# Decode attention: when the pages of the second and third set and the second rotary group are gathered

## The chip, the cores and the metric

The kernel runs on one core of a Trainium2 chip. The metric is the device time of one launch in microseconds, as the median of several runs. The five engines of the core (TensorE, VectorE, ScalarE, GpSimd and SyncE) run their own instruction streams and meet at semaphores; GpSimd and SyncE also issue the transfers. In the rows of the profile they are PE (PEld is the weight load of PE), DVE, ACT, POOL and SP.

## What is computed

One layer of a hybrid decoder: layer norm, one input projection, a gated linear attention head group, a latent attention (MLA) head group, an output projection and a gated feed-forward network with a short convolution. It is computed for a prompt of 1024 tokens with 16 meta tokens ahead of them, and for 8 decode sequences of 4 tokens. The change touches the seam between the two latent attentions:

```python
# prompt: causal attention per head over the prompt's own keys
s = (einsum('bthc,bsc->bhts', ql, ckv) + einsum('bthr,bsr->bhts', qr, krope)) * MLA_SCALE
p = softmax(where(kpos <= pq, s, NEG_INF));  o = einsum('bhts,bsc->bthc', p, ckv)
...
# decode: 8 sequences, 4096 past positions each, held in pages of 128 positions
past_ckv = cache_ckv[page_table].reshape(Bd, -1, MLA_KV_LORA)     # 256 wide
past_kr  = cache_krope[page_table].reshape(Bd, -1, MLA_ROPE)      # 32 wide
s_past = einsum('bthc,bsc->bhts', q_lat, past_ckv) + einsum('bthr,bsr->bhts', q_rope, past_kr)
p = softmax(concatenate([s_past * MLA_SCALE, s_new], -1))
o = einsum('bhts,bsc->bthc', p[..., :P], past_ckv) + einsum('bhts,bsc->bthc', p[..., P:], ckv_new)
```

All arithmetic is fp32.

## The kernel before

The program is one hand-ordered list of instructions per engine, in eight stages (a to h). Stage d is the attention over the prompt, stage e the attention of the decode tokens over the paged cache. There is no scheduler: the order on an engine is the order of the code, and an engine goes on when the semaphore that it waits for has come to its count.

**Stage d** has `N_ATT` = 66 score steps. Steps 0 and 1 are the last query rows of all heads. Steps 2 to 65 go through four passes of 16 steps; pass p takes heads 2p and 2p+1 over the eight query tiles in the order 7, 0, 6, 1, 5, 2, 4, 3. PE computes the scores of a step (L1298) and counts it in `score_done`; DVE takes the row maxima (L1419), ACT the exponentials (L1359), PE turns the probabilities (L1312), ACT and DVE copy them out, and PE multiplies them with the values (L1335). So heads 0 to 3 have been read for the last time when `score_done` is 34, and all heads when it is 66.

**Stage e** goes through `SETS` = 16 sets. A set is four sequences by 512 positions, loaded as four gathers (pieces b = 0 to 3) on the queue of POOL; each gather reads 128 rows of 4 KB, so 512 KB, into one quarter of a ring slot `ring_c` (L1564, `load_latents`). There are three slots. Slot 0 lies apart; slot 1 lies over the queries `qT` of heads 0 to 3, slot 2 over those of heads 3 to 7. `slot_free` (L1545) holds the loads of a set back until its slot is free: set 1, and by POOL's order all behind it, until `score_done` is 66; set z of 3 and more until the values of set z-3 are computed (`spv_done`). The rotary keys come in four groups of four sets (`load_rotary`, L1568), each in four gathers of 256 KB into `ring_r`, whose slots lie over tensors that are dead before the scores begin. DVE packs one set's share of a group into `ring_p` (L1859).

For a set, PE turns the pages in two parts of `turn_set` (L1652; the first part needs pieces 0 and 1, semaphore `set_loaded`, and ends with the packed rotary keys and the first block of piece 2, which needs `late_loaded`, pieces 2 and 3). ACT and DVE copy the turned blocks out, and PE computes the scores (L1673, `ss_done`) and the values (L1699). This repeats once a set.

What orders the loads in `pool_e` (L1590 to L1616): set 0 during the projections of stage d, the first rotary group at the end of them, the second rotary group when `score_done` is 33, sets 1 and 2 at the end of the scores, set 2 also after `ss_done` is 2 (the two score steps over the new tokens). From set 3 on the four pieces of a set are spread: piece 0 when the slot is free, piece 1 after the scores of set z-2, piece 2 after three, piece 3 after six of the nine turned blocks of set z-1. SP loads the output projection's weights beside this (L1578).

Of the kernel before, what the change touches and what calls it, by code (L numbers as in the profile page):

```python
# [102 lines left out]
def build(nc, ins, outs):  # L103
    with ExitStack() as ctx:
# [8 lines left out]
        def sem(name):  # L113
            return ctx.enter_context(nc.semaphore(name))
# [935 lines left out]
        def out_of_psum(eng, key):  # L1050

            eng.wait_ge(prep_act, act_at[index[key] + 1])
            if dve_at[index[key] + 1]:
                eng.wait_ge(prep_dve, dve_at[index[key] + 1])
# [177 lines left out]
        score_done = sem("score_done")  # L1232
# [14 lines left out]
        N_ATT, N_JOBS = len(att_steps), len(att_jobs)  # L1247
# [239 lines left out]
        SLOTS = 3  # L1487
        SETS = DEC_B // 4 * N_PAGES // 4
# [49 lines left out]
        def step_of(z):  # L1538
            return z + 2
# [5 lines left out]
        def slot_free(eng, z):  # L1545
            if z == 0:

                eng.wait_ge(prep_done, index[("ckv", NT - 1)] + 1)
                eng.wait_ge(latent_stored, 96)
            if z == 1:  # L1550

                eng.wait_ge(score_done, N_ATT)
            if z >= SLOTS:

                eng.wait_ge(spv_done, step_of(z - SLOTS) + 1)

        def rows_of(z, b):
            j = 2 * (4 * (z // 8) + b) + z % 8 // R_SETS
            return bass.IndirectOffsetOnAxis(ap=row_at[:, j, z % R_SETS:z % R_SETS + 1], axis=0)

        def load_latents(z, pieces=range(4)):
            for b in pieces:
                done = (set_loaded if b < 2 else late_loaded)[z % SLOTS]
                nc.gpsimd.indirect_dma_start(ring_c[z % SLOTS][:, b, :, :].rearrange("p j c -> p (j c)"), None,  # L1564
                                             ins["cache_ckv"].rearrange("n (p j) c -> (n p) (j c)", j=4),
                                             rows_of(z, b)).then_inc(done, 16)

        def load_rotary(q, pieces=range(4)):  # L1568
            for b in pieces:
                j = 2 * (4 * (q // 2) + b) + q % 2  # L1570
                nc.gpsimd.indirect_dma_start(ring_r[q % R_SLOTS][b // 2][:, b % 2, :, :].rearrange("p m c -> p (m c)"), None,
                                             ins["cache_krope"].rearrange("n (p j) c -> (n p) (j c)", j=16),
                                             bass.IndirectOffsetOnAxis(ap=rope_at[:, j:j + 1], axis=0)
                                             ).then_inc(rope_loaded[q % R_SLOTS], 16)
# [15 lines left out]
        def pool_e(pool):  # L1590
            pool.wait_ge(pages_ready, 2)
            slot_free(pool, 0)
            load_latents(0)
            out_of_psum(pool, prep[-1])
            load_rotary(0)
            pool.wait_ge(score_done, N_ATT // 2)
            load_rotary(1)
            for z in range(1, SETS):
                slot_free(pool, z)
                if z == 2:  # L1600
                    pool.wait_ge(ss_done, 2)
                if z < SLOTS:
                    load_latents(z)
                    continue
                load_latents(z, (0,))
                if 4 <= z < 12:
                    q = 1 + z // 4
                    if z % 4 == 0:
                        pool.wait_ge(rope_packed, R_SETS * (q - 1))
                    load_rotary(q, (z % 4,))  # L1610
                pool.wait_ge(ss_done, step_of(z - 2) + 1)
                load_latents(z, (1,))
                pool.wait_ge(past_turned, N_TURN * (z - 1) + 3)
                load_latents(z, (2,))
                pool.wait_ge(past_turned, N_TURN * (z - 1) + SPLIT_TURN)
                load_latents(z, (3,))  # L1616
# [1486 lines left out]
        @block.gpsimd  # L3103
        def _(pool):
            pool_ab(pool)
            pool_c(pool)
            pool_e(pool)
            pool_f(pool)
            pool_g(pool)
            pool_h(pool)  # L3110

            for i in range(XS):
                pool.wait_ge(h_stored[i], 16 * (3 if i == 0 else 2))
            pool.wait_ge(state_stored, 32)
            pool.wait_ge(last_state_stored, 16)
            pool.wait_ge(latent_stored, 96 + 48)
            nc.gpsimd.drain().then_inc(end, 1)
# [26 lines left out]
```

## Times and profile before

| what | us |
|---|---|
| median of 3 runs | 1561.29 |
| lowest and highest of them | 1558.99 and 1563.45 |
| the profiled execution, its own time | 1547.4 |
| span of the profiled execution, first to last instruction | 1545.6 |
| PE busy in it | 1479.5 |

The profile is of one execution. Its own time is 1547.4 us, of which 1.8 lie outside the span. It is 13.9 us below the median of the timed runs. All durations below are of this execution; times of day in it count from the first instruction.

### The profile page before, as it was taken

The numbers are of one execution on the slowest core, as the hardware profiler recorded it, in microseconds if no ns is written. First come the engines' busy times: TensorE is split into PE (matmuls) and PEld (weight loads), VectorE is DVE, ScalarE is ACT, GpSimd is POOL, SyncE is SP. The second block draws the span as 40 slices with busy tenths as digits, with TensorE's granted clock in tenths as the row PEclk, the third lists the DMA queues.
The fourth block names the chain that finished last, engine by engine and source line by source line (L and its number), as shares of the span: only waits on it lengthen the run. The fifth ranks groups of instructions, "written<-read, shape, count | busy, mean of one in ns | idle before, by whom it ended". The sixth has DMA issues, their size and how long they took to land.

```text
span 1545.6 us, 29086 instructions
## 1 busy us (share of the span) xinstructions
PE 1479.5 (96%) x11025; PEld 1253.8 (81%) x11025; DVE 1000.2 (65%) x1730; ACT 659.5 (43%) x1236; POOL 364.3 (24%) x395
## 2 busy tenths in 40 slices
PE   5999999999899999999999999999999999999995
PEld 5989999656566666666888999999999998778884
DVE  6714411765555555556678888888888984356587
ACT  2255422543356653334223644555554442435340
POOL 2101000210000014440111244444444442110006
PEclk9999999899899999999999999999999999999998
DMA  7221101200101037774223355555555547978552
GB/s 253 93 70 60 55 28 42 73 28 32 41 2 28 1 126 250 244 253 166 82 95 98 111 180 174 191 183 171 174 180 178 173 167 246 356 248 307 171 191 109
DMA packets 121349, 217.63 MB, mean 141 GB/s; under 512 B 10938, under 2 KB 67896, under 8 KB 118408
## 3 DMA queue, kind: packets, MB, share of 16 engines
q1 hardware_dynamic: 98138, 120.89, 24.3%
q0 software_dynamic: 22976, 95.43, 17.8%
q8 instruction: 62, 1.02, 0.3%
q14 instruction: 29, 0.24, 0.0%
q10 hardware_dynamic: 144, 0.07, 0.0%
HBM read 165.66 MB, written 50.69 MB: 140 GB/s over the span
## 4 chain that ended last, share of the span: by engine, by line
PE 62%; DVE 6%; issue 2%; ACT 2%; DMA 1%; POOL 0%; SPq 0%; DVEq 0%; ACTq 0%; POOLq 0%
PE ps L2312 9%; PE ps L2311 9%; PE ps L2310 9%; PE ps L1298 4%; PE ps L2971 3%; PE ps L2973 3%; PE ps L2972 3%; PE ps L1673 3%; PE ps L210 2%; PE ps L211 2%; PE ps L212 2%; PE ps L1335 2%; PE ps L1652 2%; PE ps L1699 2%; PE ps L1312 2%
## 5 line engine op out<-in xcount | busy, mean ns | idle before, releaser
L2310 PE MATMUL ps<-t_hi,op_hi 128*128 128x266 f32 (+1 forms) x672 | 192.3, 286 | 2.4 <-DVE gap_hi L2534 2.4
L2312 PE MATMUL ps<-t_hi,op_lo 128*128 128x266 f32 (+1 forms) x672 | 192.8, 287 | 0.0
L2311 PE MATMUL ps<-t_lo,op_hi 128*128 128x266 f32 (+1 forms) x672 | 192.7, 287 | 0.0
L210 PE MATMUL ps<-w_hi,hT_hi 128*128 128x256 f32 (+2 forms) x504 | 141.9, 282 | 3.3 <-DVE hT_lo L327 3.3
L2312 PE MATMUL ps<-h1T_hi,op_lo 128*128 128x266 f32 x504 | 144.1, 286 | 0.0
L2311 PE MATMUL ps<-h1T_lo,op_hi 128*128 128x266 f32 x504 | 143.4, 285 | 0.0
L2310 PE MATMUL ps<-h1T_hi,op_hi 128*128 128x266 f32 x504 | 143.4, 284 | 0.0
L212 PE MATMUL ps<-w_hi,hT_lo 128*128 128x256 f32 (+2 forms) x504 | 141.1, 280 | 0.0
L211 PE MATMUL ps<-w_lo,hT_hi 128*128 128x256 f32 (+2 forms) x504 | 141.1, 280 | 0.0
L2767 DVE TENSOR_TENSOR ring_lo<-d_raw,ring_hi 128x1024 fp32r<-128x1024 f32 x77 | 93.5, 1223 | 60.2 <-ACT ring_hi L2763 59.2
L2763 ACT ACTIVATE ring_hi<-d_raw 128x1024 fp32r<-128x1024 f32 x77 | 81.6, 1060 | 114.6 <-DMA d_raw<-t_res 58.9
L2310 PEld LDWEIGHTS ps<-t_hi,op_hi 128*128 128x128 f32 x672 | 127.6, 190 | 2.6 <-DVE gap_hi L2534 2.6
L2311 PEld LDWEIGHTS ps<-t_lo,op_hi 128*128 128x128 f32 x672 | 127.8, 190 | 0.0
L2312 PEld LDWEIGHTS ps<-t_hi,op_lo 128*128 128x128 f32 x672 | 127.4, 190 | 0.0
L2971 PE MATMUL ps<-ring_hi 128*128 128x512 f32 x308 | 122.3, 397 | 4.1 <-DVE ring_lo L2767 3.3
L2972 PE MATMUL ps<-ring_lo,ring_hi 128*128 128x512 f32 x308 | 120.7, 392 | 0.0
L2973 PE MATMUL ps<-ring_hi,ring_lo 128*128 128x512 f32 x308 | 120.6, 392 | 0.0
L2435 DVE TENSOR_TENSOR op_lo<-s_sum,op_hi 128x512 fp32r<-128x512 f32 x84 | 106.1, 1302 | 0.0
L1564 POOL DMA_INDIRECT ring_c<-in_cache_ckv,row_at x64 | 60.2, 940 | 177.1 <-PE ps L1298 69.9
L210 PEld LDWEIGHTS ps<-w_hi,hT_hi 128*128 128x128 f32 x504 | 97.0, 192 | 3.8 <-DVE hT_lo L327 3.7
L212 PEld LDWEIGHTS ps<-w_hi,hT_lo 128*128 128x128 f32 x504 | 97.2, 193 | 0.0
L211 PEld LDWEIGHTS ps<-w_lo,hT_hi 128*128 128x128 f32 x504 | 96.7, 192 | 0.0
(369 smaller groups left out, 3583.2 us busy)
## 6 DMA issues: line engine op xcount, KB each, us to landing
f_raw<-in_w_ffn_in SPq DMA_DIRECT2D x88, 256.0 KB, 3.4
g_res<-gap_lo SPq DMA_DIRECT2D x22, 528.0 KB, 3.6
g_mix<-in_w_down POOLq DMA_DIRECT2D x11, 1024.0 KB, 5.3
t_res<-g_mix POOLq DMA_DIRECT2D x11, 1024.0 KB, 4.2
g_mix<-g_res POOLq DMA_DIRECT2D x11, 1024.0 KB, 5.3
s_res<-g_mix POOLq DMA_DIRECT2D x11, 1024.0 KB, 4.2
d_raw<-in_w_down SPq DMA_DIRECT2D x22, 512.0 KB, 7.2
d_raw<-s_res SPq DMA_DIRECT2D x44, 256.0 KB, 3.7
```

The source lines that it names most:

```text
L210: nc.tensor.matmul(out, ah, bh, start=start, stop=False)
L211: nc.tensor.matmul(out, ah, bl, start=False, stop=False)
L212: return nc.tensor.matmul(out, al, bh, start=False, stop=stop)
L2310: nc.tensor.matmul(o, ah, bh, start=FIRST_IN[q] and k == 0, stop=False, skip_group_check=again)
L2311: nc.tensor.matmul(o, ah, bl, start=False, stop=False, skip_group_check=again)
L2312: last = nc.tensor.matmul(o, al, bh, start=False, stop=k == 3, skip_group_check=again)
L2435: nc.vector.tensor_tensor(op_lo[q][:, :, :], OP_OF[q], op_hi[q][:, :, :].bitcast(F32), sub).then_inc(op_split, 1)
L2763: nc.scalar.activation(ring_hi[m % RING][:, :], d_raw[raw_slot[m]][:, 0:1024], ACT.Copy).then_inc(d_high, 1)
L2767: nc.vector.tensor_tensor(ring_lo[m % RING][:, :], d_raw[raw_slot[m]][:, 0:1024], ring_hi[m % RING][:, :].bitcast(F32), sub).then_inc(d_sp ...
L2971: nc.tensor.matmul(b, ah, bh, start=j == 0 and not again, stop=False, skip_group_check=again)
L2972: nc.tensor.matmul(b, ah, bl, start=False, stop=False, skip_group_check=again)
L2973: last = nc.tensor.matmul(b, al, bh, start=False, stop=j == NJ - 1, skip_group_check=again)
```

## The change

`slot_free` lets set 1 go when `score_done` is 35 and asks for all 66 steps only for set 2. The four gathers of the second rotary group, which went one behind the other when `score_done` was 33, now go one at a time at 33, 36, 39 and 42. The four gathers of set 1 go one at a time at 46, 50, 54 and 58. Set 2 loses its exception: its pieces are now spread by the rule of the later sets. The number of gathers and what each of them moves stay as they are, and so does where it is put.

```diff
@@ slot_free
             if z == 1:
 
+                eng.wait_ge(score_done, 2 + N_ATT // 2)
+            if z == 2:
                 eng.wait_ge(score_done, N_ATT)
@@ pool_e
-            pool.wait_ge(score_done, N_ATT // 2)
-            load_rotary(1)
-            for z in range(1, SETS):
+            for b in range(4):
+                pool.wait_ge(score_done, N_ATT // 2 + 3 * b)
+                load_rotary(1, (b,))
+            slot_free(pool, 1)
+            for b in range(4):
+                pool.wait_ge(score_done, N_ATT // 2 + 13 + 4 * b)
+                load_latents(1, (b,))
+            for z in range(2, SETS):
                 slot_free(pool, z)
                 if z == 2:
                     pool.wait_ge(ss_done, 2)
-                if z < SLOTS:
-                    load_latents(z)
-                    continue
                 load_latents(z, (0,))
```

The order of the queue of POOL, from the second rotary group to the third set. `ring_r10` and `ring_r11` are the two halves of the second rotary slot, `ring_c0` to `ring_c2` the slots of the sets. Before:

```order
L1571 DMA ring_r10_154<-in_cache_krope,rope_at_99 128x512 [waits score_done]
L1571 DMA ring_r10_154<-in_cache_krope,rope_at_99 128x512
L1571 DMA ring_r11_155<-in_cache_krope,rope_at_99 128x512 x2
L1564 DMA ring_c1_150<-in_cache_ckv,row_at_98 128x1024 [waits score_done]
L1564 DMA ring_c1_150<-in_cache_ckv,row_at_98 128x1024 x3
```

The same place in the changed kernel, whose lines lie two lower in the file (L1566 and L1573 for L1564 and L1571):

```order
L1573 DMA ring_r00_152<-in_cache_krope,rope_at_99 128x512
L1573 DMA ring_r01_153<-in_cache_krope,rope_at_99 128x512 x2
L1573 DMA ring_r10_154<-in_cache_krope,rope_at_99 128x512 [waits score_done] x2
L1573 DMA ring_r11_155<-in_cache_krope,rope_at_99 128x512 [waits score_done] x2
L1566 DMA ring_c1_150<-in_cache_ckv,row_at_98 128x1024 [waits score_done] x4
```

The order of the gathers is the same; each of the eight now has its own count of `score_done` ahead of it, where two waits stood ahead of the eight.

The queue of POOL at the third and fourth set, which is where the exception for the third goes. Before:

```order
L1564 DMA ring_c2_151<-in_cache_ckv,row_at_98 128x1024 [waits ss_done]
L1564 DMA ring_c2_151<-in_cache_ckv,row_at_98 128x1024 x3
L1564 DMA ring_c0_149<-in_cache_ckv,row_at_98 128x1024 [waits spv_done]
L1564 DMA ring_c0_149<-in_cache_ckv,row_at_98 128x1024 [waits ss_done]
L1564 DMA ring_c0_149<-in_cache_ckv,row_at_98 128x1024 [waits past_turned] x2
```

And in the changed kernel:

```order
L1566 DMA ring_c2_151<-in_cache_ckv,row_at_98 128x1024 [waits ss_done,score_done]
L1566 DMA ring_c2_151<-in_cache_ckv,row_at_98 128x1024 [waits ss_done]
L1566 DMA ring_c2_151<-in_cache_ckv,row_at_98 128x1024 [waits past_turned] x2
L1566 DMA ring_c0_149<-in_cache_ckv,row_at_98 128x1024 [waits spv_done]
L1566 DMA ring_c0_149<-in_cache_ckv,row_at_98 128x1024 [waits ss_done]
L1566 DMA ring_c0_149<-in_cache_ckv,row_at_98 128x1024 [waits past_turned] x2
```

Three of the third set's four gathers have waits of their own now, of the kind that the fourth set's have. On PE, DVE, ACT and SP nothing moves.

## Rows read from the trace of the kernel before

**Rows 1.** The page: busy time of each engine, and the granted clock in 40 slices.

```profile
PE 1479.5 (96%) x11025; PEld 1253.8 (81%) x11025; DVE 1000.2 (65%) x1730; ACT 659.5 (43%) x1236; POOL 364.3 (24%) x395
...
PEclk9999999899899999999999999999999999999998
```

**Rows 2.** Waits of PE, 553 to 720 us: waiting <- releaser: total, times, longest.

```profile
PE ps L1652 <- ACT pastT L1757: 3.6, 15, 0.3
PE ps L1673 <- DVE catT L1465: 0.9, 1, 0.9
PE ps L1699 <- DVE oacc L1877: 0.7, 1, 0.7
```

**Rows 3.** Timeline of POOL: start, duration, engine, line, what, idle before and releaser.

```profile
556.77 0.94 POOL L1564 DMA_INDIRECT ring_c<-in_cache_ckv,row_at  x1 [69.93 <-PE ps L1298]
558.02 0.94 POOL L1564 DMA_INDIRECT ring_c<-in_cache_ckv,row_at  x1 [0.31 <-issue]
...
564.31 0.94 POOL L1564 DMA_INDIRECT ring_c<-in_cache_ckv,row_at  x1 [2.87 <-PE ps L1673]
...
568.04 0.94 POOL L1564 DMA_INDIRECT ring_c<-in_cache_ckv,row_at  x1 [0.30 <-issue]
...
583.09 0.93 POOL L1564 DMA_INDIRECT ring_c<-in_cache_ckv,row_at  x1 [1.78 <-PE ps L1673]
...
586.46 0.94 POOL L1564 DMA_INDIRECT ring_c<-in_cache_ckv,row_at  x1 [1.00 <-PE ps L1652]
```

**Rows 4.** Timeline of PE, with the same columns, 510 to 596 us.

```profile
510.91 0.91 PE L1298 MATMUL ps<-kT,qT 96*128 96x384 f32 x2
...
538.44 0.70 PE L1298 MATMUL ps<-kT,qT 96*128 96x256 f32 x2
...
573.00 1.97 PE L1652 MATMUL ps<-consts,ring_c 128*128 128x128 f32 x16
...
582.72 1.97 PE L1652 MATMUL ps<-consts,ring_c 128*128 128x128 f32 x16
...
585.56 0.63 PE L1652 MATMUL ps<-consts,ring_c 128*128 128x128 f32 x4 [0.24 <-ACT pastT L1757]
...
592.43 1.97 PE L1652 MATMUL ps<-consts,ring_c 128*128 128x128 f32 x16
...
595.27 0.63 PE L1652 MATMUL ps<-consts,ring_c 128*128 128x128 f32 x4 [0.24 <-ACT pastT L1757]
```

**Rows 5.** Line 1564, all of it, then 556 to 562 us: duration, issue to landing.

```profile
L1564 POOL DMA_INDIRECT ring_c<-in_cache_ckv,row_at x64: 932/937/1077, 342.5 to 703.0; - x64
...
DMA to landing us min/median/max: 4.2/5.2/7.7
...
L1564 POOL DMA_INDIRECT ring_c<-in_cache_ckv,row_at x4: 934/938/942, 556.8 to 560.5; - x4
...
DMA to landing us min/median/max: 4.4/5.8/6.0
```

**Rows 6.** Stretches: length, busy (x instructions) PE, PEld, DVE, ACT, POOL; clock, DMA share, GB/s.

```profile
443.35:479.40 36.05, 35.65 (x273) 24.57 (x273) 20.52 (x64) 21.86 (x56) 0.00 (x0) 1.00 0.01 1
479.40:515.46 36.06, 35.67 (x274) 24.59 (x273) 20.61 (x64) 21.86 (x56) 3.78 (x4) 1.00 0.11 30
...
572.99:582.71 9.72, 9.46 (x100) 5.92 (x96) 5.58 (x12) 3.62 (x8) 0.93 (x1) 1.00 0.35 108
582.71:592.42 9.71, 9.47 (x100) 5.92 (x96) 5.60 (x12) 3.62 (x8) 4.70 (x5) 1.00 0.79 254
...
706.36:716.07 9.71, 9.47 (x101) 5.93 (x96) 6.53 (x13) 7.29 (x12) 0.00 (x0) 1.00 0.62 233
```

**Rows 7.** Timeline of DVE: the packing of the rotary keys.

```profile
570.81 0.50 DVE L1859 COPY ring_p<-ring_r 128x256 f32<-128x256 f32 x2
...
580.73 0.70 DVE L1859 COPY ring_p<-ring_r 128x256 f32<-128x256 f32 x2
```

**Rows 8.** Groups of DVE by shape, 443.35 to 479.40 us: busy us, mean ns, idle before.

```profile
L1447 DVE COPY rs<-rinv 128x128 f32<-128x128 f32 x8 | 1.8, 227 | 0.3
```

## The prediction

> **What bounds the kernel now.** I read the page first. PE is busy 96% of the span at a granted clock of nine tenths or more in nearly every slice [rows 1], so a transfer is worth something only where PE stands still for it. So I looked next at the stage in which the moved gathers are used, by the waits of PE from the last prompt scores to the end of the decode sets. The reader is to see what is missing there [rows 2]: in 167 us PE waits 3.6 us in fifteen pieces for a copy of ACT, 0.9 once for the last output of the prompt, 0.7 once for a copy of DVE, and never for a gather. Third, the two timelines side by side. POOL issues the four gathers of the second set from 556.77 us on and those of the third from 564.31 to 568.04 [rows 3]; PE begins to turn the second set at 573.00, with no idle time ahead of it, and the third at 582.72, again with none [rows 4]. Last, the stretches: one set costs PE 9.71 to 9.72 us, whether it is the second, the third or the last [rows 6]. The sets go at the pace of PE, and that of the prompt passes, 36.05 us each, too.
>
> **The change, part by part.** The base is the profiled execution, 1547.4 us.
>
> *Second set, loaded earlier.* In the kernel before, its second gather is issued at 558.02 [rows 3], and the four land 4.4 to 6.0 us after their issue [rows 5], so pieces 0 and 1 are in by 558.02 + 6.0 = 564.0. PE needs them at 573.00 [rows 4]. The slack is 9.0 us already. The changed kernel issues the set's pieces behind score steps 46, 50, 54 and 58. Step 46 is the one at 510.91, which lasts 0.91, so 511.8; step 58 is that at 538.44 with 0.70, so 539.1 [rows 4]. With 7.7 us, the slowest landing of all 64 [rows 5], the set is whole by 546.9, and the slack grows from 9 to 26 us. A slack that grows is worth 0. What is late next is nothing, because nothing was late: PE comes to the pages in its own order after the scores and values of the set ahead.
>
> *What these gathers meet in the prompt passes.* Four issues of 0.94 us on POOL and 2 MB of transfers now lie beside passes in which ACT and DVE feed PE closely. The trace has no latent gather there, so I bound the cost. The nearest row is the pass in which the four rotary gathers go out: it holds 3.78 us of POOL and lasts 36.06 us, the pass ahead of it holds none and lasts 36.05 [rows 6]. That is 0.01 us for four issues. For the size of the transfers the nearest rows are two sets: one with five issues and 254 GB/s takes 9.71 us, the last one with no issue 9.71 too [rows 6]. The upper end is that DVE stands for the whole of each issue and PE waits for it: 4 x 0.94 = 3.8 us. A gain is excluded below 0 since no work of PE, DVE or ACT is taken away. I take 0.0, by the pass with four issues, and keep 3.8 for the range.
>
> One row does show DVE and POOL touching each other. The pair of packing copies takes 0.50 us where POOL is still and 0.70 us behind an issue at the next set [rows 7]. The prompt passes have eight copies of that kind, SBUF to SBUF, of 0.227 us each, 1.8 us in a pass of 36.05 [rows 8], so an issue mostly misses them; if every one of the four hit one at that price, it would be 4 x 0.2 = 0.8 us. *The Trainium skill*, "SBUF — State Buffer", section "Who interferes with whom", has a rule that speaks against the change: GpSimd and VectorE share one pair of SBUF ports under an exclusive lock, a VectorE copy in a two-port mode and a GpSimd instruction shut each other out for the whole instruction. By that rule a collision would cost up to one whole issue and four of them the 3.8 us above; by the row it costs 0.2. I go by the row for the sum; the rule is the third rival below.
>
> *Second rotary group, spread.* The same four issues go at 33, 36, 39 and 42 score steps in place of 33 alone. They are used after set 3, beyond 592.43 [rows 4]. The price is between 0 and the 0.01 us that they cost as a bunch; 0.
>
> *Third set, loaded later.* Its piece 0 waits for two score steps of stage e as before, so it stays at 564.31 [rows 3]. Pieces 1 to 3 move from within 568.04 to the places of the later sets. For the fourth set these are 583.09 and 586.46 for pieces 1 and 3 [rows 3], with PE's turning of the set ahead starting at 582.72 [rows 4], so 0.37 and 3.74 us behind that start. The third set's come 0.37 and 3.74 behind 573.00: 573.4 and 576.7. PE needs the first at 582.72 and the last two at 585.56 [rows 4], leads of 9.3 and 8.8 us. The slowest landing of all is 7.7 [rows 5], so 1.1 us are left at the tightest point. The fourth set lives with the same lead: 592.43 - 583.09 = 9.34 and 595.27 - 586.46 = 8.81 [rows 3, 4], and so do the twelve behind it; the 0.24 us ahead of the second is a wait for ACT, which the third set has as well. The cost is 0; the cover is PE's set of 9.71 us, and without it each microsecond of landing beyond 8.8 would be paid once. The burst of eight gathers between 556 and 573 goes away; it held nobody, so it gives nothing.
>
> *The waits that are added* stand on POOL alone. What is queued behind them is POOL's own next gather, and nobody else: POOL idles 69.93 us ahead of 556.77 [rows 3]. The last of set 1 is out at 540, long before the third set's turn, and the last of the third set at 577.7, before the fourth's slot comes free.
>
> **The sum.** 1547.4 + 0 + 0 + 0 + 0 = 1547.4 us for an execution like the profiled one. The profiled one is 13.9 us under the median of the timed runs; the change takes nothing off either, so I forecast the median, 1561.3.
>
> **The rivals.**
>
> *Faster: the second set is late in the timed runs.* The 13.9 us between the profile and the median are unexplained, and gathers that land late could be part of them. PE would wait for the second set from a landing of 573.00 - 558.02 = 15.0 us on, and the change would give back what is beyond that. For 4.7 us, which is 0.3%, landings of 19.7 us are needed. Against it: thirteen later sets have leads of 8.8, so each would wait 10.9, 142 us in all, ten times the difference that there is. It would give some 1556. Chance 3%.
>
> *Slower: the third set is late.* It changes a lead of 17 us (585.56 less 568.04) for one of 8.8. From a landing of 8.8 us on PE waits at the third set, once, and the thirteen later sets wait as they did before. For: 1.1 us of room in this profile, and a w_o transfer beside it. Against: the stretch of the third set carries only 108 GB/s before, and those of the later sets take 254 without a wait [rows 6]. Landings of 14 us in the timed runs would give 1561.3 + 5.2 = 1566.5. Chance 3%.
>
> *Slower within the noise: DVE stands for POOL in the passes.* One whole issue for each of four gathers, 1561.3 + 3.8 = 1565.1. For: the 0.2 us at the packing copies. Against: the two passes at 36.05 and 36.06. Chance 4%.
>
> **How the numbers follow.** The forecast keeps 90%. A difference under 0.3%, some 4.7 us, is about what a measurement of this kernel can't tell from no change. The third rival lies within that, so within 0.3% is 90 + 4 = 94%, faster 3%, slower 3%. The range takes the three runs' own spread, 1559.0 to 1563.5, widened to the 3.8 us bound on both sides since a new median of few runs moves by as much as that spread: 1557.5 to 1565.1.
>
> **What would show it right or wrong.** Right: in the changed kernel's timeline POOL issues the second set at about 512, 520, 530 and 539 us, and the third set's last three near 573.4 to 576.7; PE still turns the second set at 573.0 and the third at 582.7; the passes stay at 36.05 and PE's waits still name no gather. The third rival would show as passes of 37 to 38 us and longer copies at L1447; the second as idle time of PE ahead of 582.7 or 585.6. The forecast is wrong if PE's turning of set two moves ahead of 573.0: then something did hold the seam that I don't see.

## The result and the profile after

The change measured faster: 1550.93 us (median of 14 runs, 1547.43 to 1558.13) against 1556.02 (14 runs, 1552.77 to 1563.45). The ratio is 0.9963, with a 95% interval of 0.9948 to 0.9978, so about 5.8 us less. The forecast was 1561.3 in a range of 1557.5 to 1565.1 and no difference.

The profile of the changed kernel shows none of this. It spans 1545.7 us, where that of before spans 1545.6. Its own time, 1547.43 us, is the lowest of the changed kernel's 14 runs. The timeline of POOL in the changed kernel (start, duration, engine, line, what, idle before and releaser) has the gathers where the prediction put them [rows 3]:

```profile
482.29 0.94 POOL L1573 DMA_INDIRECT ring_r<-in_cache_krope,rope_at  x1 [79.69 <-PE ps L1298]
...
503.50 0.94 POOL L1573 DMA_INDIRECT ring_r<-in_cache_krope,rope_at  x1 [5.96 <-PE ps L1298]
512.74 0.94 POOL L1566 DMA_INDIRECT ring_c<-in_cache_ckv,row_at  x1 [8.30 <-PE ps L1298]
...
539.56 0.94 POOL L1566 DMA_INDIRECT ring_c<-in_cache_ckv,row_at  x1 [8.34 <-PE ps L1298]
564.91 0.94 POOL L1566 DMA_INDIRECT ring_c<-in_cache_ckv,row_at  x1 [24.41 <-PE ps L1677]
573.47 0.94 POOL L1566 DMA_INDIRECT ring_c<-in_cache_ckv,row_at  x1 [7.62 <-PE ps L1677]
...
576.84 0.94 POOL L1566 DMA_INDIRECT ring_c<-in_cache_ckv,row_at  x1 [1.00 <-PE ps L1656]
```

PE, in the same kernel and columns, turns the second set at 573.10 and the third at 582.82, as before but for 0.1 us [rows 4]. The one new thing comes in the fourth set's turn, beside the gathers of the fifth, where PE waits 0.35 us at 594.85:

```profile
573.10 1.97 PE L1656 MATMUL ps<-consts,ring_c 128*128 128x128 f32 x16
...
582.82 1.97 PE L1656 MATMUL ps<-consts,ring_c 128*128 128x128 f32 x16
...
592.53 1.97 PE L1656 MATMUL ps<-consts,ring_c 128*128 128x128 f32 x16
594.85 0.63 PE L1656 MATMUL ps<-consts,ring_p 128*128 128x128 f32 x4 [0.35 <-DVE pastT L1753]
...
602.59 1.97 PE L1656 MATMUL ps<-consts,ring_c 128*128 128x128 f32 x16
```

The stretches (length, busy us of PE, PEld, DVE, ACT and POOL, granted clock, DMA share, GB/s) keep their 36.05 and 9.71 us [rows 6], with the gathers now in the prompt passes:

```profile
479.40:515.46 36.06, 35.66 (x276) 24.59 (x272) 20.62 (x64) 21.83 (x56) 4.72 (x5) 1.00 0.14 36
515.46:551.51 36.05, 35.65 (x276) 24.59 (x272) 20.38 (x64) 21.93 (x56) 2.82 (x3) 1.00 0.17 54
...
572.99:582.71 9.72, 9.46 (x100) 5.92 (x96) 5.58 (x12) 3.62 (x8) 3.75 (x4) 1.00 0.65 204
```

Two equal profiles and two unequal medians: the profiled execution of before took 1547.4 us, and its timed runs 1552.77 at best, so it must be of a kind that they are not of. So the first thing to get was another profile of the kernel before.

### The profile page after: what moved, and what is told of

It reads as the page before. It is cut to its first block, busy times and chain, and to the rows that moved or that the text cites. A ratio compares the mean times of both kernels' runs of the same rounds, so it can differ in the third digit from the quotient of the medians.

```text
span 1545.7 us, 29088 instructions
## 1 busy us (share of the span) xinstructions
PE 1478.8 (96%) x11025; PEld 1252.7 (81%) x11025; DVE 1001.4 (65%) x1730; ACT 659.4 (43%) x1236; POOL 365.2 (24%) x395
## 4 chain that ended last, share of the span: by engine, by line
PE 62%; DVE 5%; issue 3%; DMA 2%; ACT 1%; POOL 0%; SPq 0%; DVEq 0%; ACTq 0%; POOLq 0%
PE ps L2316 9%; PE ps L2315 9%; PE ps L2314 9%; PE ps L1298 4%; PE ps L1656 3%; PE ps L1677 3%; PE ps L2975 3%; PE ps L2977 3%; PE ps L2976 3%; PE ps L210 2%; PE ps L211 2%; PE ps L212 2%; PE ps L1335 2%; PE ps L1312 2%; PE ps L1703 2%
## 5 line engine op out<-in xcount | busy, mean ns | idle before, releaser
L1566 POOL DMA_INDIRECT ring_c<-in_cache_ckv,row_at x64 | 60.1, 940 | 161.3 <-PE ps L1677 46.8
```

## Experiments

The kernels of one group ran on one chip, beside runs of the kernel before on that chip. The groups fell on four chips, numbered 7, 4, 6 and 1 here; the chip of the result above is not recorded. A ratio is against before on the same chip.

### The same two kernels again, and one part of the change at a time (chip 7)

`before_again` and `after_again` are the two kernels unchanged. The other two do one part alone. `set1_early` has the second set spread over the passes, but not the second rotary group, and the third set in its burst:

```diff
--- before
+++ set1_early
+                eng.wait_ge(score_done, 2 + N_ATT // 2)
+            if z == 2:
                 eng.wait_ge(score_done, N_ATT)
...
-            for z in range(1, SETS):
+            slot_free(pool, 1)
+            for b in range(4):
+                pool.wait_ge(score_done, N_ATT // 2 + 13 + 4 * b)
+                load_latents(1, (b,))
+            for z in range(2, SETS):
```

```diff
--- before
+++ set2_spread
-                if z < SLOTS:
+                if z < 2:
                     load_latents(z)
                     continue
```

> The kernel before, letter for letter, timed against itself: the size of a difference that is none. Both theories expect a ratio of 1.000 within 0.0015 and a profiled span of 1545 to 1556 us. If it lies 0.003 or more off 1, the measured 0.9963 of the change says nothing. Its profile may also catch one of the longer executions (the timed runs of before lay at 1552.8 to 1563.5 us, its profile at 1547.4), and so show in which stretch the extra 5 to 16 us lie.

> The changed kernel again. Theory A, the gain is real and comes with the seam: ratio 0.995 to 0.998 again. Theory B, the change does nothing and 0.9963 was drift between executions: ratio 0.999 to 1.001. The forecast on record is B.

> Only the second set's pages go out early, one at a time at 46, 50, 54 and 58 score steps; the second rotary group stays in one bunch and the third set in one burst behind the two new-token score steps. Theory A1, the gain is that the second set's pages are not in the burst of eight at 556 to 573 us: ratio as the whole change, 0.996. Theory A2, the gain comes from the third set's spreading: 0.999 to 1.001. Theory B: 0.999 to 1.001. In the profile PE is to begin the second set at 573 us under all of them.

> Only the third set's pieces are spread by the rule of the later sets; the second set still goes in one burst of four when all scores are done, and the rotary group in one bunch. Theory A1: 0.999 to 1.001, or a part of the gain since the burst is four in place of eight. Theory A2: 0.996. Theory B: 0.999 to 1.001. In the profile the third set's last three gathers are to stand at 573.4 to 576.7 us.

| kernel | median us | ratio, 95% interval | profiled span |
|---|---|---|---|
| before, 32 runs | 1558.90 | | |
| before_again | 1557.85 | 0.9999 (0.9980 to 1.0018) | 1561.6 |
| after_again | 1551.18 | 0.9949 (0.9928 to 0.9970) | 1552.8 |
| set1_early | 1556.20 | 0.9986 (0.9967 to 1.0006) | 1551.9 |
| set2_spread | 1557.74 | 0.9990 (0.9974 to 1.0007) | 1557.3 |

The gain is real and repeats. Each part alone gave less, and neither is clear of no difference. And `before_again` gave the profile that was missing. The waits of PE in it, 553 to 720 us, against [rows 2]:

```profile
PE ps L1652 <- issue: 3.3, 13, 0.4
PE ps L1321 <- issue: 1.9, 1, 1.9
PE ps L1699 <- DVE oacc L1877: 1.5, 1, 1.5
...
PE ps L1335 <- ACT ptb L1379: 0.7, 1, 0.7
```

In the first profile of before the wait at L1699 was 0.7 us, at L1335 there was none, and at L1321 PE waited this long:

```profile
560.82 0.33 PE L1321 MATMUL ps<-consts,rs 128*128 128x128 f32 x1 [0.57 <-DVE rs L1447]
```

Where they come from is seen on three engines of `before_again` at once, POOL, PE and ACT:

```profile
562.35 0.94 POOL L1564 DMA_INDIRECT ring_c<-in_cache_ckv,row_at  x1 [69.93 <-PE ps L1298]
...
566.09 0.94 POOL L1564 DMA_INDIRECT ring_c<-in_cache_ckv,row_at  x1 [0.30 <-issue]
```

```profile
563.91 1.31 PE L1335 MATMUL ps<-ptb,v_h 128*64 128x128 f32 x20
565.16 0.66 PE L1312 MATMUL ps<-consts,probs 128*128 128x128 f32 x4
567.72 0.33 PE L1321 MATMUL ps<-consts,rs 128*128 128x128 f32 x1 [1.91 <-issue]
568.79 1.98 PE L1335 MATMUL ps<-ptb,v_h 128*64 128x128 f32 x16 [0.74 <-ACT ptb L1379]
```

```profile
566.66 0.28 ACT L1387 ACTIVATE rb<-ps 128x128 f32<-128x128 f32 x1 [2.16 <-PE ps L1335]
568.14 0.60 ACT L1379 ACTIVATE ptb<-ps 128x512 f32<-128x512 f32 x1 [1.19 <-remote]
```

PE's L1335 ends at 563.91 + 1.31 = 565.22. ACT, which has nothing else to do and waits for its signal, starts at 566.66, 1.4 us later; in the profile of before the same copy starts 0.05 us behind the same matmul, 558.34 + 1.31 = 559.65:

```profile
558.34 1.31 PE L1335 MATMUL ps<-ptb,v_h 128*64 128x128 f32 x20
559.70 0.28 ACT L1387 ACTIVATE rb<-ps 128x128 f32<-128x128 f32 x1 [0.77 <-PE ps L1335]
```

PE's L1312 ends at 565.8, and ACT takes its result at 568.14. DVE waits for ACT's copy before it writes the next row sums (`rs`), and PE's L1321 waits for those. The trace also records when each semaphore is incremented. The latest four places, set against the end of the instruction that increments it, and the medians between 395 and 725 us of `before_again`:

```
semaphore increments: landing time (us), behind the end of its instruction, behind each issue of POOL before it
566.64  PE L1335  1.41 late   4.30 3.05 1.79 0.55
568.11  PE L1312  2.30 late   5.77 4.52 3.27 2.02
493.45  PE L1298  1.22 late   5.73 4.48 3.23 1.98
579.02  PE L1652  0.83 late   5.75 4.51 3.26 2.02
median of PE 0.014, of ACT 0.008, of DVE 0.010; largest of ACT 0.01, of DVE 0.02
```

Only PE's signals are late. The ends of matmuls are modelled in the profile, so the trace does not tell whether the increment is held back or the end of the matmul itself; that ACT starts late, it tells. The long delays stand behind a bunch of four issues, and the last ones of a bunch land at one point, 5.7 to 5.9 us behind the first issue and 2.0 to 2.2 behind the fourth. (Smaller ones stand elsewhere: 0.68 us behind the first rotary group, 4.2 us behind its first issue, and 0.3 to 0.4 in five decode sets.) It holds on this chip behind each of the bunches from 480 us on: behind the second rotary group in `before_again`, `set1_early` (1.21) and `set2_spread` (1.18), behind the second set in `before_again` (2.30) and `set2_spread` (2.29), behind the third in `before_again` (0.83) and `set1_early` (2.21). In the first profile of before, with the same three bunches, the latest signal of PE is 0.07 us late. The profile of the changed kernel has the small ones, 0.68 us behind the first rotary group and up to 0.39 in the sets. So it is of an execution with late signals, and that of before is not.

The second rotary group's bunch holds nobody up all the same. In `before_again` it goes out from 487.71 us on, and the pass around it lasts 512.68 - 476.62 = 36.06 us, as in the first profile:

```profile
476.62 1.56 PE L1298 MATMUL ps<-kT,qT 96*128 96x512 f32 x4
...
512.68 1.56 PE L1298 MATMUL ps<-kT,qT 96*128 96x512 f32 x4
```

Then the clock. The stretches of `before_again`, with the columns as above:

```profile
560.00:565.00 5.00, 4.38 (x46) 3.15 (x44) 1.99 (x9) 3.51 (x10) 2.05 (x3) 1.00 0.17 39
565.00:570.00 5.00, 2.35 (x23) 1.77 (x19) 0.59 (x3) 0.87 (x2) 1.73 (x2) 0.82 0.91 306
570.00:575.00 5.00, 4.14 (x66) 3.51 (x63) 2.57 (x10) 1.14 (x6) 1.43 (x2) 0.50 0.25 87
575.00:580.00 5.00, 3.86 (x38) 3.16 (x36) 3.00 (x6) 2.58 (x6) 2.33 (x3) 0.99 0.89 274
580.00:585.00 5.00, 4.60 (x32) 0.82 (x32) 1.33 (x5) 0.00 (x0) 0.00 (x0) 0.69 0.62 244
```

PE is busy 2.35 of the 5 us from 565, and in the next 5 us the granted clock is 0.50, the 1.2 GHz level of the two; it falls a second time behind the third set's bunch, to 0.69 over five us. From the start of the last matmul of the prompt scores (L1298) to the first at L2100, past all sixteen sets, before takes 190.6 us in its first profile and 199.0 in this one: 8.4 us more. Of these PE's longer waits at the seam are 1.91 + 0.74 - 0.57 at L1321 and L1335 and 1.54 - 0.72 at L1699, 2.9 us together. Most of the rest is PE at the lower clock: the clock missing in the five stretches from 565 to 590 us (the last has 0.97) is worth 5 x (0.18 + 0.50 + 0.01 + 0.31 + 0.03) = 5.2 us at most, an estimate.

The profile of `before_again` is 16.0 us longer than the first one. Besides the 8.4 us at the seam, 4.0 lie ahead of the first prompt score, 1.5 among the prompt scores, all in the first part of them, where the signal behind the first rotary group is 0.68 us late, and 2.0 behind L2100. The change touches none of these, and what makes them was not looked for.

| profile | latest signal of PE behind a bunch of four from 480 us on | last L1298 to first L2100 (its line in that kernel) |
|---|---|---|
| before | 0.07 | 190.6 |
| before_again | 2.30 | 199.0 |
| set2_spread | 2.29 | 197.2 |
| set1_early | 2.21 | 195.9 |
| after_again | no bunch left | 193.1 |
| after | no bunch left | 192.2 |

Each bunch at the seam makes a hole of its own, behind which the clock falls: to 0.50 from 570 us in `set2_spread`, to 0.76 in `set1_early`. Without the second set's bunch the stretch is 3.1 us shorter, without the third's 1.8, without both 5.9. By these profiles the parts nearly add up. In the times, 0.0014 and 0.0010 against 0.0051, they add up to less, but each ratio has an interval of 0.0017 to 0.0021 to either side, so whether the whole is more than its parts stays open. The profiles are of one execution each, too: that of `before_again` is 5.6 us above its kernel's median, that of `after_again` 3.3 above its own.

### What in a bunch does it (chip 4)

Four variants of the changed kernel: the second set as one bunch in the middle of a pass; spread, but late, at the seam; a bunch of four small gathers at the old place, beside the changed order; and no bunch, but ACT held up by hand.

```diff
--- after
+++ set1_bunch_in_pass
-            for b in range(4):
-                pool.wait_ge(score_done, N_ATT // 2 + 13 + 4 * b)
-                load_latents(1, (b,))
+            pool.wait_ge(score_done, N_ATT // 2 + 13)
+            load_latents(1)
```

```diff
--- after
+++ set1_spread_at_seam
-            for b in range(4):
-                pool.wait_ge(score_done, N_ATT // 2 + 13 + 4 * b)
-                load_latents(1, (b,))
+            pool.wait_ge(score_done, N_ATT)
+            load_latents(1, (0,))
+            pool.wait_ge(rs_ready, N_JOBS)
+            load_latents(1, (1,))
+            pool.wait_ge(ss_done, 2)
+            load_latents(1, (2,))
+            pool.wait_ge(past_turned, 5)
+            load_latents(1, (3,))
...
+                if z == 2:
+                    pool.wait_ge(past_turned, 9)
```

```diff
--- after
+++ after_small_burst
...
+            pool.wait_ge(score_done, N_ATT)
+            for b in range(4):
+                nc.gpsimd.indirect_dma_start(small[:, b, :], None,
+                                             ins["cache_ckv"].rearrange("n p (x c) -> (n p x) c", c=64),
+                                             rows_of(1, b)).then_inc(small_done, 16)
...
```

```diff
--- after
+++ after_act_delay
...
+                if k == N_ATT - 1:
+                    act_settle(nc.scalar.activation(idle_copy[:, :], wide[:, 0:SEQ], ACT.Copy))
+                    act_settle(nc.scalar.activation(idle_copy[:, :], wide[:, 0:SEQ], ACT.Copy))
                 if k - 2 in job_of_last:
                     r_copy(job_of_last[k - 2])
```

> The changed kernel, but the second set's four gathers go as one bunch when 46 score steps are done, in the middle of a prompt pass (about 512 to 516 us). Theory S (stall beside a bunch): in some executions four 512 KB gathers in one bunch hold ACT and DVE up for 1 to 2 us some 3 us after the first of them, PE runs dry, and its granted clock falls to half for a few us. Then this bunch costs here too: ratio 0.997 to 0.999 and, if the profiled execution is one of those, a pass of 37 us or more in place of 36.05 and a clock under 1 near 520. Theory P (place): only the end of the prompt attention is thin enough for a gap of PE; then the ratio is that of the change, 0.995 to 0.996, and the pass stays at 36.05. If the rotary bunch of 4 x 256 KB, which held up nothing in six profiles, is the pattern, P.

> The changed kernel, but the second set's gathers go at the end of the prompt scores and in the first steps of stage e, as before, only one at a time: behind 66 score steps, behind the last row sums, behind the two new-token scores and behind five turned blocks; the third set follows. Theory S: no bunch, no stall, ratio 0.995 to 0.997 as the change. Theory E (earliness): the gain is that the pages are there early, or that nothing but compute lies at the seam; then 0.998 to 1.000.

> The changed kernel with four further gathers in one bunch at the place where the second set's stood before (66 score steps done), each of 128 rows of 256 bytes in place of 4 KB, into scratch. The issues of POOL and their number of rows are those of the old bunch, the bytes a sixteenth. Theory D (data): what holds ACT and DVE up is the transfer of 2 MB, so nothing happens: ratio 0.995 to 0.996. Theory I (issue): POOL's four issues hold them up; then 0.998 to 0.999 and idle time of ACT or DVE of 1 to 2 us behind the bunch in the profile.

> The changed kernel with two copies of 128x1024 on ACT, 1.1 us each, right ahead of the last copy but one of the row-sum reciprocals, the instruction that came 1.4 us late in the long execution of before. It makes by hand the delay of 2.2 us, in every execution and without a bunch of gathers. Theory C (clock): the hole in PE's work lets its granted clock fall to half at 565 to 575 us, and the delay costs more than its own length: 4 to 7 us, ratio 0.998 to 1.000 against before. Without the clock's part it would cost 2.2 us or less, ratio 0.9965 to 0.9975.

The kernels measured:

| kernel | median us | ratio, 95% interval | last L1298 to first L2100 |
|---|---|---|---|
| before, 35 runs | 1557.42 | | |
| set1_bunch_in_pass | 1556.01 | 0.9991 (0.9972 to 1.0009) | 192.1 |
| set1_spread_at_seam | 1551.00 | 0.9963 (0.9947 to 0.9979) | 192.2 |
| after_small_burst | 1556.93 | 0.9988 (0.9969 to 1.0006) | 197.4 |
| after_act_delay | 1555.70 | 0.9993 (0.9978 to 1.0008) | 196.6 |

The changed kernel itself was not in this group; `set1_spread_at_seam` stands for it. The intervals of the ratios overlap a little, so the argument rests on the last column and the rows as well.

*The place does not matter, the bunch does.* In `set1_bunch_in_pass`, ACT and then PE in the pass:

```profile
520.33 0.28 ACT L1387 ACTIVATE rb<-ps 128x128 f32<-128x128 f32 x1 [3.93 <-remote]
...
521.43 1.91 PE L1298 MATMUL ps<-kT,qT 96*128 96x512 f32 x2 [2.39 <-ACT probs L1359]
```

PE's signal for that copy lands 2.87 us late, 5.7 us behind the first issue. The clock is 0.66 from 520 to 525 us, and the stretch of the prompt scores takes 154.5 us where the changed kernel takes 150.2. All 4.3 us of it lie beside the bunch: sixteen matmuls of the scores take 16.4 us there in place of 12.1. `set1_spread_at_seam` puts the same four gathers at 556.20, 560.40, 563.18 and 565.49, where the bunch stood, and from there up to the third set no signal of PE is over 0.05 us late, the clock stays at 1.00, and the ratio is like that of the change on the other chips. So being early is not what the change gains by.

*The bytes do not matter.* The small gathers of `after_small_burst` move a sixteenth, and their two late signals are those of the full bunch: 1.42 and 2.28 us late, 4.30 and 5.75 us behind the first issue. The number of rows is the same as before, so the issues and what is made for each row are not told apart. Its DMA engines are nearly idle meanwhile (DMA share 0.14), and the clock falls as well:

```profile
565.00:570.00 5.00, 2.87 (x30) 2.16 (x30) 0.87 (x5) 1.66 (x5) 3.10 (x4) 1.00 0.14 26
570.00:575.00 5.00, 3.42 (x70) 2.93 (x70) 1.87 (x9) 1.50 (x6) 0.16 (x1) 0.71 0.01 3
575.00:580.00 5.00, 5.00 (x30) 4.99 (x29) 2.29 (x4) 2.07 (x6) 0.78 (x1) 0.61 0.35 105
```

*The hole, not the gather, lets the clock fall.* In `after_act_delay` no bunch and no late signal stands at the seam, only 2.1 us of copies on ACT. PE waits 1.8 us at L1321 where it waited 0.6, is busy 3.18 of 5 us, and then the granted clock is 0.56:

```profile
560.00:565.00 5.00, 3.18 (x44) 2.49 (x42) 0.59 (x3) 3.45 (x6) 0.00 (x0) 1.00 0.00 0
565.00:570.00 5.00, 4.14 (x66) 3.67 (x63) 2.57 (x10) 1.64 (x6) 0.94 (x1) 0.56 0.03 7
```

That delay takes the whole gain away: 0.9993 where the spread kernel beside it has 0.9963, so 0.0030 x 1557 = 4.7 us for 2.1 us of work, by two ratios with 0.0015 and 0.0016 to either side. From the last prompt score to L2100 it takes 196.6 us, against 192.2: 4.4 us more, for a wait of PE that is 1.3 us longer.

### The other bunches (chip 6)

`rotary_spread` is before with the second rotary group spread alone. The other three change the changed kernel further: `set1_in_pairs` issues the second set as two pairs, at 46 and 54 score steps. `first_rotary_spread` issues the first rotary group at 6, 12, 18 and 24 score steps. `no_pairs` adds to the last that a rotary gather of the later groups no longer stands 1.25 us behind the first piece of a set but behind its last:

```diff
--- before
+++ rotary_spread
-            load_rotary(1)
+            for b in range(4):
+                pool.wait_ge(score_done, N_ATT // 2 + 3 * b)
+                load_rotary(1, (b,))
```

```diff
--- after
+++ set1_in_pairs
-            for b in range(4):
+            for b in range(0, 4, 2):
                 pool.wait_ge(score_done, N_ATT // 2 + 13 + 4 * b)
-                load_latents(1, (b,))
+                load_latents(1, (b, b + 1))
```

```diff
--- after
+++ no_pairs (its first edit alone: first_rotary_spread)
-            load_rotary(0)
+            for b in range(4):
+                pool.wait_ge(score_done, 6 + 6 * b)
+                load_rotary(0, (b,))
...
                 load_latents(z, (3,))
+                if 4 <= z < 12:
+                    q = 1 + z // 4
+                    if z % 4 == 0:
+                        pool.wait_ge(rope_packed, R_SETS * (q - 1))
+                    pool.wait_ge(past_turned, N_TURN * z)
+                    load_rotary(q, (z % 4,))
```

The same lines go away behind piece 0.

> The kernel before with one part of the change alone: the second rotary group one gather at a time at 33, 36, 39 and 42 score steps. In three of four profiles with this group in a bunch, two of PE's semaphore signals landed 0.8 and 1.2 us late, 5.7 to 5.8 us behind the first issue of the bunch. Theory S: these two are gone, the pass keeps its 36.05 us, the bunches at the seam still cost; gain 0 to 1.2 us, ratio 0.998 to 1.000. Theory P (only the seam matters): 1.000.

> The changed kernel, but the second set's gathers go as two pairs, at 46 and at 54 score steps. How large must a bunch be? In the decode sets PE's signal behind a pair 1.25 us apart lands 0.35 to 0.4 us late. If the delay grows with the number of issues close together, a pair holds a signal up for some 0.4 us in the pass, and the ratio stays at 0.995 to 0.997; if any bunch is as bad as four, signals 1.4 to 2.9 us late, and 0.998 to 0.999.

> The changed kernel with one more bunch undone: the first rotary group's four gathers go at 6, 12, 18 and 24 score steps in place of in a bunch at the end of the projections, where in nine of ten profiles PE's signal of the first tail scores lands 0.7 us late. Theory S: that signal comes in time, gain 0.5 to 1 us and perhaps a shorter stretch at the half clock at 395 to 410 us: ratio against before 0.993 to 0.996. Theory P: as the change, 0.995 to 0.996.

> As first_rotary_spread, and the rotary gathers of the later groups no longer stand 1.25 us behind the first piece of a set but behind its last, when the set ahead is turned. In the changed kernel PE's score signal lands 0.35 to 0.4 us late in up to eight sets (those with a rotary gather) and in no other. Theory S: none is late, up to 8 x 0.35 = 2.8 us less: ratio against before 0.992 to 0.995, and sets of 9.71 us throughout. If the pairs don't matter, as first_rotary_spread.

All four came out at no difference: 0.9999 (0.9988 to 1.0011), 0.9993 (0.9983 to 1.0004), 1.0001 (0.9990 to 1.0012) and 1.0000 (0.9988 to 1.0013). But before itself ran at 1548.8 us on this chip, 9 to 10 less than on the other two, and in all four profiles, `rotary_spread` with its bunches at the seam among them, no signal of PE between 395 and 725 us is over 0.07 us late. This chip does not have the effect, and so these four said nothing on the size of a bunch. They said something else, and a second group, which fell on chip 6 again, asked it directly:

> The changed kernel once more, beside the three below. Theory S holds for chips where PE's signals land late behind POOL's issues: where before runs at 1555 us or more, ratio 0.995 to 0.997; where before runs at 1550 or less, as on chip 6, 0.999 to 1.001.

> The second rotary group alone is spread. On a chip with late signals: the two signals that landed 0.8 and 1.2 us late behind this bunch come in time, gain 0 to 1.2 us of some 1558, ratio 0.998 to 1.000, since the bunches at the seam are left. On a chip without: 1.000.

> The second set's gathers in two pairs in the pass. On a chip with late signals: if the delay grows with the issues that stand close together, signals 0.3 to 0.5 us late behind each pair and a ratio as the change, 0.995 to 0.997; if a pair is as bad as four, 1.4 to 2.9 us late and 0.998 to 0.999. On a chip without: 1.000.

> The changed kernel with the first rotary group spread and the later rotary gathers taken out of the pairs. On a chip with late signals: no signal later than 0.1 us in the whole stage, up to 0.7 + 8 x 0.35 = 3.5 us less than the change, ratio 0.992 to 0.996. On a chip without: 1.000.

The change itself is worth nothing there: `after_third` has 0.9994 (0.9982 to 1.0006) against before at 1548.39, and the others 0.9989 (0.9978 to 1.0000), 0.9993 (0.9983 to 1.0004) and 0.9995 (0.9983 to 1.0007). From the last prompt score to L2100 `after_third` takes 190.5 us and `rotary_spread_2` 190.6, what before takes in its first profile. That profile is like chip 6 in every number: 1545.6 us, no late signal, 190.6.

### A last pair on a chip with the effect (chip 1)

> The second set's gathers in two pairs in the pass. On a chip with late signals (before at 1555 us or more): if the delay grows with the issues that stand close together, signals 0.3 to 0.5 us late behind each pair and a ratio of 0.995 to 0.997; if a pair is as bad as four, 1.4 to 2.9 us late and 0.998 to 0.999. On a chip without (before at 1550 or less): 1.000 and no late signal.

> The changed kernel with the first rotary group spread and the later rotary gathers taken out of the pairs. On a chip with late signals: no signal later than 0.1 us in the stage, ratio 0.992 to 0.996. If spreading further than the change does gives nothing: 0.995 to 0.996. On a chip without: 1.000.

Before ran at 1557.08 (11 runs), `set1_pairs_3` at 1549.24, ratio 0.9946 (0.9931 to 0.9962), and `no_pairs_3` at 1547.19, ratio 0.9936 (0.9920 to 0.9953). The change itself was not run here. This chip has the effect: behind the first rotary group, still a bunch in `set1_pairs_3`, a signal of PE lands 0.61 us late, where the median of PE is 0.014. The same bunch gives 0.66 to 0.69 on chips 7 and 4. Behind the two pairs in the pass no signal is over 0.1 us late, so a pair costs nothing there. In the decode sets a rotary gather that stands 1.25 us behind a set's first piece does: up to 0.37 us in this profile, 0.39 and 0.40 in the two of the change. That is the 0.35 us at 594.85 in the rows of after above, a set of 602.59 - 592.53 = 10.06 us in place of 9.71. In `no_pairs_3` the latest signal of all is 0.28 us late, where none over 0.1 was expected, and PE waits in the stage for nothing over 0.9 us:

```profile
PE ps L1659 <- ACT pastT L1764: 2.6, 11, 0.3
PE ps L1659 <- issue: 0.9, 4, 0.2
PE ps L1680 <- DVE catT L1465: 0.9, 1, 0.9
PE ps L1706 <- DVE oacc L1884: 0.7, 1, 0.7
```

It takes 190.5 us from the last prompt score to L2100, as on chip 6, where the change takes 192.2 and 193.1, and it spans 1543.6, the shortest of all profiles. It beats the kernel before on this chip, and its median of 1547.19 is no longer above what before takes on chip 6 (1548.4 and 1548.8): the difference between the chips is gone with the bunches and pairs. That it beats `set1_pairs_3`, and with it the change, is likely by its profile, but the two ratios of this group overlap, so the timing alone does not show it.

## Why the prediction was wrong

**What bounds the kernel.** PE, yes, and for the trace that was read each number held: the second set is not waited for, the third is not late, the passes keep 36.05 us with the gathers in them. The eight places in the timeline came out within 0.9 us. (Rows 2 leave out two waits of 0.6 us, at L1312 and L1321; they change none of this.)

**The step that failed** is the one on the third set: "The burst of eight gathers between 556 and 573 goes away; it held nobody, so it gives nothing." In the trace that I had it held nobody. In `before_again` on chip 7 it holds PE's signals back, up to 2.3 us behind its first four gathers and 0.8 behind its last four, and PE's clock falls behind each. In its place stand 5.9 to 6.8 us: 199.0 us from the last prompt score to L2100 with the bunches, 193.1 and 192.2 without. The measured gain is 5.8 us, and 7.9 when repeated (0.0051 x 1558).

**The base** was off as well. The forecast of 1561.3 lies 10.4 us above the measured median of 1550.9. Of these 5.3 belong to the kernel before, whose median was 1561.29 by three runs and 1556.02 by fourteen, and 5.1 to the change.

**The clue was on the page.** "The 13.9 us between the profile and the median are unexplained", and every timed run was more than 11 us above the profiled one. I weighed one explanation, late landings, found that it could be no more than a small part, and gave what was left the price of nothing. The right reading was that the profile might not be of the kind of execution that was timed, so that every "nobody waits here" in it was open by up to 13.9 us somewhere, and that the range had to reach down for a change that moves gathers. The sum on such a base is right for the base alone.

**"A gain is excluded below 0 since no work of PE, DVE or ACT is taken away"** was wrong as a rule. A hole in PE's work can go without any work going, and it can count more than its length: 2.1 us of delay on ACT made PE wait 1.3 us longer and cost 4.4 to 4.7.

**The rivals.** The faster one had 3% and the wrong mechanism: in `before_again` too PE waits for no gather. The slower one, the third set, stayed away, and so did DVE standing for POOL: DVE's signals are never over 0.02 us late, and a pass with 4.72 us of POOL in it takes 36.06. The price of the rotary group, "between 0 and the 0.01 us that they cost as a bunch", came from the same trace, and it was right in part by luck: on chip 7 the bunch makes two signals land 0.8 and 1.2 us late, but the pass with it keeps its 36.06 us. What its spread alone is worth was timed on chip 6 only, where it is nothing clear of noise (0.9999 and 0.9989).

## What to carry to other kernels

Where the profiled execution lies far below every timed run, the profile can be of another kind of execution: look for a profile whose time is near the median before costing anything, above all before writing "it held nobody". Issue the gathers of GpSimd a few microseconds apart rather than issuing four in a bunch, even where nobody waits for the data, and compare a suspect wait with the end of the instruction that should have released it. A hole in the work of TensorE can cost more than its length when its clock falls behind it.

## What the runs showed of the hardware

Behind four indirect gathers that GpSimd issues 1.25 us apart, semaphore increments of TensorE's matmuls land up to 2.9 us late against the profile's end of the matmul, the last of them 5.7 to 5.9 us behind the first issue, for gathers of 512 KB, 256 KB and 32 KB (`set1_bunch_in_pass`, `before_again`, `after_small_burst`). Behind the first rotary group's bunch it is 0.61 to 0.69 us. Increments of VectorE and ScalarE are not touched (0.02 us at most). Two gathers 1.25 to 1.4 us apart go with 0.3 to 0.4 us in the decode sets, once 0.6 (`set1_bunch_in_pass`), and with nothing in a prompt pass; gathers 2.3 us and more apart with at most 0.13. In `no_pairs_3` two signals are 0.28 us late behind gathers 1.4 to 2.3 us apart. Chips 7, 4 and 1 showed it, chip 6 not at all: eight profiles have no increment later than 0.07 us, and before runs 9 to 10 us faster. What in the chip holds the increments back, whether gathers that are not indirect do it, and why one chip does not show it, these runs do not tell.

The granted clock of TensorE went down behind a hole in the engine's work, whether a late signal or a delay made by hand had made it. In `before_again` the engine was busy 2.35 of 5 us, at a clock of 0.82, and 0.50, the 1.2 GHz level, followed; in `after_small_burst` it was busy 2.87 us at 1.00, and 0.71 and 0.61 followed; in `after_act_delay` 3.18 us at 1.00, and 0.56 and 0.76 followed. The values are means over five microseconds each.
